# An encoder layer on one core: the recurrence branch's projection by seven block products per pair of column blocks

## What is computed

```python
h = x @ w_in                                   # 8192 columns: u, v, q, two f, i, g, gate_a, gate_b
a = gmlp_branch(u_a, v_a, ...) @ w_pa          # w_pa: 512 x 1024
r = hgrn2_branch(q, f_fwd, f_bwd, ...) @ w_pb  # w_pb: 1024 x 1024
mixed = sigmoid(gate_a) * a + sigmoid(gate_b) * r
x = layer_norm(ALPHA * x + mixed @ w_o, ln1_g, ln1_b)
y = moe_ffn(x, ...)                            # 64 routed experts, top 6, one shared expert
return layer_norm(ALPHA * x + y, ln2_g, ln2_b)
```

## Time and profile before

| | before |
|---|---|
| median of 3 runs | 1757.95 us (1757.85 to 1760.21) |
| the profiled execution | 1757.98 us |
| its span in the profile | 1756.1 us |
| TensorE busy | 1672.5 us, 95% |
| TensorE's weight loads busy | 830.0 us, 47% |
| VectorE busy | 653.8 us, 37% |
| ScalarE busy | 330.0 us, 19% |
| GpSimd busy | 136.8 us, 8% |

### The profile page before, as it was taken

One profiled execution on the slowest core, in us unless ns is written; L12 is line 12 of the kernel. 1 busy time (PEld: TensorE's weight loads), 2 busy tenths in 40 slices (PEclk: granted clock), 3 DMA queues, 4 the chain that ended last, 5 costly groups with the idle time before them and its releaser, 6 DMA issues.

```text
span 1756.1 us, 23431 instructions
## 1 busy us (share of the span) xinstructions
PE 1672.5 (95%) x9569; PEld 830.0 (47%) x9569; DVE 653.8 (37%) x1039; ACT 330.0 (19%) x522; POOL 136.8 (8%) x141
## 2 busy tenths in 40 slices
PE   6999999999999999999999999999998999898967
PEld 3444455666666555555554555433333333333323
DVE  5010127888888866541113776200000000000018
ACT  1111112222222221111000220122222122111212
POOL 0000000000000000000001113311111111111100
PEclk9999999999999999999999999999999999999989
DMA  6114101101111001211126008599999999999858
GB/s 224 48 48 155 61 12 49 37 27 33 36 36 36 25 13 48 64 32 43 54 89 252 25 24 358 222 420 422 423 424 422 421 423 422 415 412 393 326 201 353
DMA packets 104990, 330.56 MB, mean 188 GB/s; under 512 B 8496, under 2 KB 64848, under 8 KB 86736
## 3 DMA queue, kind: packets, MB, share of 16 engines
q1 hardware_dynamic: 91520, 291.69, 42.3%
q0 software_dynamic: 13392, 37.77, 5.5%
HBM read 306.88 MB, written 33.55 MB: 194 GB/s over the span
## 4 chain that ended last, share of the span: by engine, by line
PE 82%; DMA 9%; DVE 7%; issue 1%; ACT 1%; SPq 0%; DVEq 0%; POOL 0%; POOLq 0%; ACTq 0%
PE pA L1129 16%; PE pg L707 11%; PE pg L734 11%; PE pB L1155 7%; PE pB L943 5%; DMA rA<-w_e_gate_up 4%; PE pg L747 2%; PE pB L992 2%; PE pA L992 2%; PE pA L935 2%; DMA rA<-y_dram 2%; PE pg L1116 2%; DMA rEF<-w_e_gate_up 2%; PE pA L840 2%; PE pA L900 1%; PE pg L900 1%
## 5 line engine op out<-in xcount | busy, mean ns | idle before, releaser
L734 PE MATMUL pg<-rA,hw 128*128 128x384 f32 x768 | 264.5, 493 | 0.7 <-ACT aTr L1265 0.7
L1129 PE MATMUL pA<-rCD,aTr 128*32 128x512 f32 (+2 forms) x720 | 208.7, 600 | 12.2 <-DMA rA<-w_e_gate_up 10.7
L1936 DVE TENSOR_TENSOR rows<-rows,pA 128x256 f32<-128x256 f32 x45 | 18.9, 421 | 532.2 <-ACT rows L1407 532.2
L707 PE MATMUL pg<-rEF,rA 128*128 128x512 f32 x448 | 194.7, 596 | 3.1 <-ACT rCD L1244 3.1
L734 PEld LDWEIGHTS pg<-rA,hw 128*128 128x128 f32 x768 | 140.2, 190 | 86.5 <-ACT aTr L1265 0.9
L707 PEld LDWEIGHTS pg<-rEF,rA 128*128 128x128 f32 x448 | 85.5, 192 | 109.6 <-issue 109.6
L1129 PE MATMUL pA<-rA,aTr 128*32 128x512 f32 (+2 forms) x384 | 123.8, 605 | 0.0
L1129 PE MATMUL pA<-rB,aTr 128*32 128x512 f32 (+1 forms) x368 | 108.9, 602 | 5.8 <-DMA rEF<-w_e_gate_up 4.1
L1129 PE MATMUL pA<-ew,aTr 128*32 128x512 f32 (+1 forms) x352 | 108.9, 612 | 0.0
L1155 PE MATMUL pB<-rCD,rows 128*32 128x512 f32 (+2 forms) x360 | 105.1, 595 | 0.0
L1129 PE MATMUL pA<-rEF,aTr 128*32 128x512 f32 (+1 forms) x352 | 101.8, 603 | 0.1
(11 more groups left out here) (382 smaller groups left out, 2348.0 us busy)
## 6 DMA issues: line engine op xcount, KB each, us to landing
rCD<-w_e_gate_up SPq DMA_DIRECT2D x21, 2048.0 KB, 30.6
rA<-w_e_gate_up SPq DMA_DIRECT2D x11, 2048.0 KB, 31.6
rB<-w_e_gate_up SPq DMA_DIRECT2D x11, 2048.0 KB, 27.7
ew<-w_e_gate_up SPq DMA_DIRECT2D x11, 2048.0 KB, 32.7
rEF<-w_e_gate_up SPq DMA_DIRECT2D x11, 2048.0 KB, 33.2
rCD<-w_e_down SPq DMA_DIRECT2D x21, 1024.0 KB, 32.4
hw<-w_in SPq DMA_DIRECT2D x36, 512.0 KB, 4.0
rA<-w_e_down SPq DMA_DIRECT2D x11, 1024.0 KB, 33.6
```

The source lines that it names most:

```text
L707: last = mm(big_bank(fill), x1T[:, c, i * P:(i + 1) * P], strip[n % 2][:, c, :], start=(c == 0), stop=(c == KC - 1))
L734: last = mm(pg[:, n * 512:n * 512 + HALF], hw3[m][:, c, :], x1T[:, c, n * HALF:(n + 1) * HALF], start=(c == 0), stop=(c == KC - 1))
L1129: last = mm(gu[n][o:o + w, :], xT[n][:, c, o:o + w], at(gate_up_home(j % NB)[0], gate_up_home(j % NB)[1] + c * F, [[2 * D, 2], [1, F]]), s ...
```

## The change

The projections go over pairs of column blocks (q = 0 to 3). Per pair, w_pa's two blocks are multiplied as before (16 matmuls, into pA and pB), and w_pb's two blocks with the scheme of the merge gates: seven products of four matmuls (`r_product`), into four banks of pX and pg that are used in turn (`proj_bank`). VectorE makes four sums of token blocks once (`proj_t`, in rCD and ew), four sums of weight blocks per pair (`proj_s`, in ew), and seven sums of products per pair (`r_sum`) in `rows`, which ScalarE's copy of product 0 starts. Then come the multiplications by the gates and the sums into `mT`, block by block. SP loads a pair of blocks at a time: w_pb's pair when all seven products of the pair before are done. w_o is loaded at the start of the stage. As `rows` and the shared expert's place are now used by the projection, w_router and the bias are loaded after the last product, and x1_back, the ln1 rows and the shared expert's weights after the last sum.

```diff
+        proj_s = [slabs(ew[:, 8 * HALF + k * 512:8 * HALF + (k + 1) * 512], 4) for k in range(4)]
+        proj_t = [slabs(r, 4) for r in (rCD[:, KC * D:KC * D + 4 * HALF], rCD[:, KC * D + 4 * HALF:KC * D + 8 * HALF],
+                                        ew[:, 0:4 * HALF], ew[:, 4 * HALF:8 * HALF])]
...
+        def rT_quarter(k, n):
+            return rT[:, 4 * k:4 * k + 4, n * HALF:(n + 1) * HALF]
...
         pair = [pA, pB]
         pairY = [pB, pX]
+
+        def proj_bank(m):
+            return (pX, pg)[m % 4 // 2][:, (m % 2) * 512:(m % 2) * 512 + HALF]
 
...
             w_pa = d["w_pa"].rearrange("(p c) n -> p c n", c=4)
             w_pb = d["w_pb"].rearrange("(p c) n -> p c n", c=KC)
             sp.wait_ge(gp_filled, 7 * (KC - 1))
-            sp.dma_start(hw3[0][:, 0:4, :], w_pa[:, :, 0:P]).then_inc(s_pa, 16)
-            sp.dma_start(hw3[1], w_pb[:, :, 0:P]).then_inc(s_pb, 16)
-            with sp.Fori(1, KC) as f:
-                sp.wait_ge(pa_filled, f)
-                sp.dma_start(hw3[0][:, 0:4, :], w_pa[:, :, bass.ds(f * P, P)]).then_inc(s_pa, 16)
-                sp.wait_ge(pb_filled, f)
-                sp.dma_start(hw3[1], w_pb[:, :, bass.ds(f * P, P)]).then_inc(s_pb, 16)
-
-            sp.wait_ge(rt_filled, NT)
-            sp.dma_start(wo_sb, d["w_o"].rearrange("(c p) n -> p c n", p=P)).then_inc(s_wo, 16)
+            for q in range(KC // 2):
+                if q:
+                    sp.wait_ge(pa_filled, 2 * q)
+                sp.dma_start(pa_w, w_pa[:, :, 2 * q * P:2 * (q + 1) * P]).then_inc(s_pa, 16)
+                if q:
+                    sp.wait_ge(pb_filled, 7 * q)
+                sp.dma_start(pb_w, w_pb[:, :, 2 * q * P:2 * (q + 1) * P]).then_inc(s_pb, 16)
+                if q == 0:
+                    sp.wait_ge(rt_filled, NT)
+                    sp.dma_start(wo_sb, d["w_o"].rearrange("(c p) n -> p c n", p=P)).then_inc(s_wo, 16)
+
+            sp.wait_ge(pb_filled, 7 * (KC // 2))
+            sp.dma_start(wr_sb, d["w_router"].rearrange("(p c) n -> p c n", c=KC)).then_inc(s_wr, 16)
+            sp.dma_start(bias[:, :], d["router_bias"].to_broadcast([P, E])).then_inc(s_wr, 16)
+            sp.wait_ge(x1_stored, 16 * NT)
+            sp.wait_ge(m_ready, KC)
+            for i in range(NT):
+                sp.dma_start(x1_back[:, i, :], d["x1_dram"][i * P:(i + 1) * P, :]).then_inc(s_x[i], 16)
+                if i == 0:
+                    sp.dma_start(rows[:, 0:D], d["ln1_g"].to_broadcast([P, D])).then_inc(s_ln1, 16)
+                    sp.dma_start(rows[:, D:], d["ln1_b"].to_broadcast([P, D])).then_inc(s_ln1, 16)
             sp.dma_start(wsh[:, :, 0:F], d["w_sh_gate"].rearrange("(p c) n -> p c n", c=KC)).then_inc(s_wsh, 16)
             sp.dma_start(wsh[:, :, F:], d["w_sh_up"].rearrange("(p c) n -> p c n", c=KC)).then_inc(s_wsh, 16)
-            sp.dma_start(rows[:, 0:D], d["ln1_g"].to_broadcast([P, D])).then_inc(s_ln1, 16)
-            sp.dma_start(rows[:, D:], d["ln1_b"].to_broadcast([P, D])).then_inc(s_ln1, 16)
-            sp.dma_start(wr_sb, d["w_router"].rearrange("(p c) n -> p c n", c=KC)).then_inc(s_wr, 16)
-            sp.dma_start(bias[:, :], d["router_bias"].to_broadcast([P, E])).then_inc(s_wr, 16)
-            sp.wait_ge(pa_filled, KC)
             sp.dma_start(wsh_d, d["w_sh_down"].rearrange("(j p) n -> p j n", p=P)).then_inc(s_wsh, 16)
-            sp.wait_ge(m_ready, KC)
-            sp.wait_ge(x1_stored, 16 * NT)
-            for i in range(NT):
-                sp.dma_start(x1_back[:, i, :], d["x1_dram"][i * P:(i + 1) * P, :]).then_inc(s_x[i], 16)
             for i in range(NT):
                 sp.wait_ge(x2_ready, i + 1)
...
+            def a_projected(q):
+                pe.wait_ge(s_pa, 16 * (q + 1))
+                for m in range(2):
+                    if q:
+                        pe.wait_ge(pa_taken, 2 * (q - 1) + m + 1)
+                    for n in range(2):
+                        for c in range(4):
+                            last = mm(pair[m][:, n * 512:n * 512 + HALF], pa_w[:, c, m * P:(m + 1) * P],
+                                      aT[:, c, n * HALF:(n + 1) * HALF], start=(c == 0), stop=(c == 3))
+                    last.then_inc(pa_filled, 1)
+
+            def r_product(q, m, a, b):
+                if m == 4:
+                    pe.wait_ge(pp_out, q + 1)
+                elif m > 4 or q:
+                    pe.wait_ge(pb_sums, 7 * (q - 1) + (4, 5, 7, 7, 0, 8, 9)[m])
+                for c in range(4):
+                    last = mm(proj_bank(m), a[:, c, :], b[:, c, :], start=(c == 0), stop=(c == 3))
                 last.then_inc(pb_filled, 1)
 
-            projections(0, True)
-            with pe.Fori(1, KC) as f:
-                projections(f)
+            for q in range(KC // 2):
+                a_projected(q)
+                pe.wait_ge(s_pb, 16 * (q + 1))
+                a, b = pb_w[:, :, 0:P], pb_w[:, :, P:2 * P]
+                s1, s2, s3, s4 = proj_s
+                t1, t2, t3, t4 = proj_t
+                r_product(q, 0, a[:, 0:4, :], rT_quarter(0, 0))
+                pe.wait_ge(pt_ready, 1)
+                pe.wait_ge(pw_ready, q + 1)
+                r_product(q, 1, s2, t2)
+                r_product(q, 2, a[:, 4:8, :], rT_quarter(1, 0))
+                r_product(q, 3, s1, t1)
+                r_product(q, 4, s4, rT_quarter(1, 1))
+                r_product(q, 5, s3, t3)
+                r_product(q, 6, b[:, 4:8, :], t4)
 
             pe.wait_ge(pa_taken, KC)
             pe.wait_ge(s_wo, 16)
...
+            for q in range(KC // 2):
+                sc.wait_ge(pb_filled, 7 * q + 1)
+                if q:
+                    sc.wait_ge(m_ready, 2 * q)
+                fn(proj[0], proj_bank(0), ACT.Copy).then_inc(pp_out, 1)
+
...
+            link(difference(p1, rT_quarter(0, 1), rT_quarter(0, 0)))
+            link(difference(p2, rT_quarter(1, 1), p1))
+            link(difference(p3, rT_quarter(1, 1), rT_quarter(0, 1)))
+            difference(p4, rT_quarter(1, 0), p2).then_inc(pt_ready, 1)
+            chain.restart()
+
+            def r_sum(q, n, m, dst, a):
+
+                ve.wait_ge(pb_filled, 7 * q + m + 1)
+                if n == 1:
+                    ve.wait_ge(pp_out, q + 1)
+                v.tensor_tensor(proj[dst], proj_bank(m), proj[a], ALU.add).then_inc(pb_sums, 1)
+                ve.wait_ge(pb_sums, 7 * q + n)
+
+            def wide(region, f):
+                return region[:, f:f + 1, :].rearrange("p a t -> p (a t)")
+
             ve.wait_ge(gate_done, 4 * (KC - 1))
-            chain.restart()
-            with ve.Fori(0, KC) as f:
-                ve.wait_ge(pa_filled, f + 1)
-                gate_a = sga[:, bass.ds(f, 1), :].rearrange("p a (n t) -> p (a n) t", n=2)
-                gate_b = sgb[:, bass.ds(f, 1), :].rearrange("p a (n t) -> p (a n) t", n=2)
-                v.tensor_tensor(slabs(ew[:, 0:T], 2), slabs(pA[:, :], 2)[:, :, 0:HALF], gate_a,
-                                ALU.mult).then_inc(pa_taken, 1)
-                ve.wait_ge(pb_filled, f + 1)
-                v.tensor_tensor(slabs(ew[:, T:2 * T], 2), slabs(pB[:, :], 2)[:, :, 0:HALF], gate_b,
-                                ALU.mult).then_inc(pb_taken, 1)
-                ve.wait_ge(pa_taken, f + 1)
-                ve.wait_ge(pb_taken, f + 1)
-                v.tensor_tensor(mT[:, bass.ds(f, 1), :].rearrange("p a t -> p (a t)"), ew[:, 0:T], ew[:, T:2 * T],
-                                ALU.add).then_inc(m_ready, 1)
-                ve.wait_ge(m_ready, f + 1)
+            ve.wait_ge(g_evicted, POST + 4)
+            for q in range(KC // 2):
+                ve.wait_ge(s_pb, 16 * (q + 1))
+                a, b = pb_w[:, :, 0:P], pb_w[:, :, P:2 * P]
+                s1, s2, s3, s4 = proj_s
+                link(v.tensor_tensor(s1, b[:, 0:4, :], b[:, 4:8, :], ALU.add))
+                link(difference(s2, s1, a[:, 0:4, :]))
+                link(difference(s3, a[:, 0:4, :], b[:, 0:4, :]))
+                difference(s4, a[:, 4:8, :], s2).then_inc(pw_ready, 1)
+                for m in range(2):
+                    ve.wait_ge(pa_filled, 2 * q + m + 1)
+                    gates = wide(sga, 2 * q + m)
+                    v.tensor_tensor(slabs(gates, 2), slabs(pair[m][:, :], 2)[:, :, 0:HALF], slabs(gates, 2),
+                                    ALU.mult).then_inc(pa_taken, 1)
+                r_sum(q, 1, 1, 2, 0)
+                r_sum(q, 2, 2, 0, 0)
+                r_sum(q, 3, 3, 1, 2)
+                r_sum(q, 4, 4, 1, 1)
+                r_sum(q, 5, 5, 2, 2)
+                r_sum(q, 6, 3, 3, 2)
+                r_sum(q, 7, 6, 2, 2)
+                ve.wait_ge(pa_taken, 2 * q + 2)
+                for m in range(2):
+                    gates = wide(sgb, 2 * q + m)
+                    link(v.tensor_tensor(gates, rows[:, 2 * m * HALF:2 * (m + 1) * HALF], gates, ALU.mult))
+                    v.tensor_tensor(wide(mT, 2 * q + m), wide(sga, 2 * q + m), gates, ALU.add).then_inc(m_ready, 1)
 
```

(30 more changed lines are left out.)

2 lines of the change are left out of this document (added).

## The result

| | before | after |
|---|---|---|
| median of the executions shown here | 1758.08 us (4: 1757.85 to 1760.21) | 1746.21 us (4: 1745.39 to 1747.30) |
| ratio | | 0.9931 [0.9917, 0.9945] |
| the profiled execution, its span | 1757.98, 1756.1 us | 1745.39, 1743.6 us |

The change is faster by 11.9 us where 10.3 were forecast. Later runs of the same two kernels on other chips widen the sample: with the four above, nine executions of the change have the median 1746.57 (1744.87 to 1750.28), and 57 of before 1758.27.

The account below looks back on a forecast made before the run. TensorE was taken to bound the kernel, busy 1672.5 of 1756.1 us. The removed matmuls gave -10.32 us and all other terms 0: 1757.98 - 10.32 = 1747.66, against the median 1747.6 us; range 1746.4 to 1750.5.

Parts of the forecast that it names:

- Matmuls, -10.32 us: Projection stage on TensorE: 16 fewer matmuls at 0.645 us each, -10.32 us, the whole gain.
- a rival: Projection stage: removed matmuls give back only about half their time, 5.1 us, so 1752.9 us; chance 0.02.
- Sums, seams, end of the stage, 0 us: Projection stage: VectorE's sums, w_pb loads at seams between pairs and the stage's last operations stay covered, 0 us.
- rival B: Seams between pairs: the single w_pb buffer stalls TensorE for landings beyond 9.9 us; 1774 us, slower; chance 0.02.
- Moved loads, 0 us: Loads moved around the projection stage, with the ln1 rows, delay nothing: 0 us, 0.3 us at the slow end.
- Rival C: Experts' stage, paced by weight loads, gives the gain back: 1758 us; chance 0.02 in full, 0.03 for a part.
- the low end of the range: Later stages: waits and half-clock tails, like one of 1.2 us, may fall otherwise by as much: 1746.4 us.
- everything later: Sign of being right: everything behind the projection stage comes 10.3 us earlier.

Follow-up runs that it names:

- the pair without waits for weights: Before and the change, each with only half of the routed experts' gate and up weights loaded: 1734.76 us and 1723.67 us.

## What was right in the prediction, and the step that failed

*Matmuls, -10.32 us.* Right: the stage measured 10.32 us less, everything up to the experts 10.2, and putting 16 matmuls back cost 10.4. A removed matmul gives back its full 0.645 us. The rows that decided it were the abutting pieces of the chain. The Trainium skill (Trainium Kernel Development and Optimization, "Performance Expectations") calls the weight loads' busy share a good measure of how close a kernel is to roofline, and matmul busy time a bad one. Read as the price of a removed matmul, as the prediction did for a rival, it would have given 5.1 us, and the 10.32 us of the stage speak against that reading.

*Sums, seams, end of the stage, 0 us.* Right: w_pb 5.9 us (forecast 4.1 to 7.3), sums ready at 8.8 (8.1 to 10.3), VectorE's last wide operation 4.5 us behind the last product (5.2). The prediction put rival B's point at landings of 9.9 us. Landings of 5.9 us cost nothing, and landings 10.8 to 11.3 us after the seam cost 4.3 us against 3.6 by its rule, so the point lies between and the rule fits. It was wrong on where TensorE would stand (product 0, not product 1) and on the tail behind a long wait: 3.2 us instead of 1.2 at each seam, so that landings of 16 us cost 27.4 us where the rule and the tails of 1.2 give 22. Rival B itself did not come about, so the forecast did not feel this.

*Moved loads, 0 us.* Right. The rows were there 13.1 us behind the last product, between the forecast of 11.8 and the upper end of 14.1 (the three loads took 8.1 us from the first issue, not 6.6), and x2_tile(0) started at 13.9. The cover was 0.7 us at the transposes: the tile was done at 938.83, they started at 939.50. It is thin, and the run with the rows in another place of the queue shows what lies behind it.

*Rival C* (the experts give the gain back) did not come about: they start 10.2 us earlier and end 12.3 us earlier in the profiled executions.

*The step that failed* is the low end of the range: "the waits and half-clock tails of the later stages, like the one of 1.2 us in the earlier trace rows, may fall otherwise by as much: 1746.4". One tail of 1.2 us was taken for the whole spread between executions. (Its 7.03 and 8.20 us are for 16 records, so for 8 matmuls; the prediction calls them 16.) The runs showed a spread of 5.4 us over nine executions of the change, with a standard deviation of 1.8 us, and 1.4 for before. A median of three or four executions is then uncertain by about 1 us, on both sides: of the before value that the sum starts from, and of the result. The centre was good (1747.6 against 1747.03 in the mean of nine, 1746.57 in their median). As an estimate from these numbers, the low end should have stood near 1745.5.

Single tails also fall otherwise by more than 1.2 us, and there are several. Two of them stand ahead of the projections, where all kernels here have the same instructions. TensorE behind a wait in the products with w_in and behind one in the gates, in the change's profiled execution

```profile
55.52 55.17 PE L725 MATMUL pg<-rEF,rA 128*128 128x512 f32 x128 [3.12 <-ACT rCD L1276]
...
693.22 2.85 PE L918 MATMUL pA<-rA,hw 128*128 128x384 f32 x8 [2.30 <-DVE rEF L1721]
```

and in that of the kernel with the matmuls put back:

```profile
55.37 56.87 PE L725 MATMUL pg<-rEF,rA 128*128 128x512 f32 x128 [3.12 <-ACT rCD L1277]
...
695.04 4.38 PE L918 MATMUL pA<-rA,hw 128*128 128x384 f32 x8 [2.56 <-DVE rEF L1722]
```

The same records behind nearly the same waits, 1.7 and 1.5 us apart. The granted clock over 54 to 60 is 1.00 of full in the first and 0.72 in the second; over the gates' eight records it is 1.00 and 0.64. So the second runs a part at the 1.2 GHz level, and its projections start 3.3 us later than the change's. In thirteen profiled executions the first piece took 56.9 us six times and 55.2 seven times, and the second 4.3 to 4.5 us four times and 2.85 nine times. The experts have four more waits of over 2 us in the change's trace (2.47 to 5.18 us, for weights). These are single executions of different kernels: that the executions of one kernel differ in just this way is likely, but not shown.

The prediction also said that "everything later" would be 10.3 us earlier, and so put the experts' stage at no gain of its own. In the profiled executions it was 2.1 us shorter, and the first late load lands 2 us earlier in each kernel whose projections are written out. What stays open: by what way a longer program text moves that landing, why the median of written-out before does not show it, and whence the 0.8 us of surplus come in the pair without waits for weights. The difference of 11.3 us between the means is, with its error of 0.6, compatible with 10.3 alone; so it is not shown that the kernel gained anything beyond its 16 matmuls. That the result fell 0.2 us outside the range was the luck of the sample: the median of all nine executions, 1746.57, lies inside it.

## What to carry to other kernels

Where the chain's pieces abut on TensorE and matmuls have one duration whatever they read, count the removed matmuls at that duration, and put the work into the seams: for each, when the buffer is free, when the load lands, when the sums stand, against when TensorE asks. Two small rows at the wrong place of a queue can take back the whole of such a gain (12 us here), so place every load behind a moved one on a time axis. And take both ends of a range from the spread of executions too, not from one event in a trace.

## What the runs showed of the hardware

Behind waits of 2.3 to 2.6 us in the gates the next eight records took 2.85 us in one execution and 4.38 in another, with a granted clock of 1.00 and 0.64. Behind 5.7 us of idle in the projections they took 5.49, twice their 2.74. Behind waits of 0.56 to 0.98 us they took 2.85, with a granted clock of 1.00.

Writing a loop out, with the same matmuls, loads and waits, moved the landing of a load 400 us later by 2 us (31.91 to 29.74), in the profiled execution. The median time of the kernel did not move.
